# The prompt's latent attention moved between the steps of a delta-rule recurrence, in a two-layer decoder step

## The chip, the cores and the metric

The kernel runs as one program on one core of a Trainium2 chip. The metric is device time in microseconds, from the start to the end of one execution. The core has five engines with one in-order queue each: PE (TensorE), DVE (VectorE), ACT (ScalarE), POOL (GpSimd) and SP (SyncE, which here only issues DMAs). They meet through semaphores. PE writes its results to eight banks of PSUM, called banks below, and DVE or ACT empties them into SBUF.

## The reference, cut to what matters

One step of a decoder with two layers, for a prompt (16 meta tokens and 256 tokens, 272 positions) and for eight samples with one new token each and a past of 1024 positions. All is float32. The change is in the odd layer, whose mixer is two things side by side: an RWKV-7 recurrence with 8 heads of 64, and multi-head latent attention (MLA) with 8 heads.

```python
def step(S, inp):                                    # RWKV-7, per head
    r_t, w_t, k_t, v_t, a_t, b_t = inp
    sa = jnp.einsum('bhij,bhj->bhi', S, a_t)
    S = S * w_t[:, :, None, :] + sa[..., None] * b_t[:, :, None, :] + v_t[..., None] * k_t[:, :, None, :]
    return S, jnp.einsum('bhij,bhj->bhi', S, r_t)
...
q = (qa @ P['mla_w_qb'][i]).reshape(B, T, MLA_HEADS, QK_NOPE + QK_ROPE)     # 64 + 32 columns a head
q_nope, q_rope = q[..., :QK_NOPE], rope(q[..., QK_NOPE:], pos)
c, kr = rms_norm(ckv, P['mla_kv_norm'][i]), rope(kr, pos)                   # latent 256, rotary key 32
q_lat = jnp.einsum('bthn,chn->bthc', q_nope, P['mla_w_uk'][i])
# samples only: past_c, past_kr gathered from 64 pages of 128 positions, put ahead of c and kr
s = (jnp.einsum('bqhc,bkc->bhqk', q_lat, c) + jnp.einsum('bqhr,bkr->bhqk', q_rope, kr)) * MLA_SCALE
pr = jax.nn.softmax(jnp.where(k_pos <= q_pos, s, -jnp.inf), axis=-1)
y_d = jnp.einsum('bthc,chv->bthv', jnp.einsum('bhqk,bkc->bqhc', pr, c), P['mla_w_uv'][i])
mix = jnp.concatenate([y_c, y_d], -1) @ P['od_w_out'][i]                    # y_c is the recurrence's side
```

## The kernel before, in words

The queues' order is written out by hand: `odd_pe`, `odd_dve`, `odd_act`, `odd_pool` and `odd_sp` hold the odd layer's instructions for each engine. PSUM's eight banks are two rings of four (`Ring`, L150): V, emptied by DVE, and A, emptied by ACT. `claim` (PE) waits until a bank of the ring is free again, `take` (DVE or ACT) until the next one is full; a ring is served strictly in order.

**The recurrence.** The prompt's 272 positions are three tiles, of 128, 128 and 16 (the tuple PT, L542). For each tile and all eight heads, PE turns four token-major operands (L546), makes five pairs of products of 128 by 128 (L564), DVE masks them and sets up the inverse of a triangular matrix (ten masks, then six operations, on which PE waits), and four *levels* build that inverse: squares (L576), masked by DVE, then two products each (L583, L587), added by DVE. Behind the levels come a product with the values (`ak`, L592), the results of L600, L606 and L620, the outputs of the tile (L629, L630), and for each 32 positions one step of the state (L638, L642). PE and DVE wait on each other all the way; ACT and, after the sample part is done, POOL have almost nothing to do there.

**Behind the recurrence** stands the whole latent attention. First the state's store (L649) and the key matrix turned (L662); queries head by head into 64 rows of a bank (L670) and the rotary parts (L676); the recurrence's head means (L1536); keys per head (L698); its variances (L1536); values (L704); latents turned (L710 to L716); the samples' latent queries (L730) and scores with the new token (L738). Then follow the prompt's eight heads: scores (L744), softmax on DVE and ACT (L1054 to L1065, L1169), probabilities turned (L805), times values (L817). Between the heads, by the tables TURNED and SCORED (L146, L147), PE turns the samples' cached keys (L756, with one set of key buffers for each third of the 288 key rows) and makes their scores (L765). At the end stand the samples' probabilities, values (L790) and output (L834), and the output projection (L1603) with the mixture of experts behind it.

The cache's 64 pages (128 KB of latents each on SP's queue, L1297, and 16 KB of rotary keys on POOL's, L1263) are loaded into SBUF columns that the recurrence uses, so both queues wait until the recurrence's operands are dead, its states stored (`wkv_out`) and the latent queries made (`qlat`). The table of pages is read for 40 of them ahead of that wait, for the last 24 between the loads.

Of the kernel before, what the change touches and what calls it, by code (L numbers as in the profile page):

```python
# [27 lines left out]
P = 128  # L28
# [9 lines left out]
NPG = PAST // PAGE  # L38
ALPHA = 4.0 ** 0.25
# [106 lines left out]
TURNED = {2: [(0, 0)], 3: [(0, 1), (0, 2)], 4: [(1, 0), (1, 1)], 5: [(1, 2), (2, 0)], 6: [(2, 1), (2, 2)], 7: [(3, 0), (3, 1), (3, 2)]}  # L146
SCORED = {3: 0, 5: 1, 6: 2, 7: 3}  # L147
# [45 lines left out]
SCRATCH = 30820  # L193
# [26 lines left out]
def program(nc, a, outs):  # L220
    sems = {}

    with ExitStack() as ctx:
# [23 lines left out]
        h_full, h_free, g_full, g_free = sem("h_full"), sem("h_free"), sem("g_full"), sem("g_free")  # L247
        v_full, v_free, a_full, a_free = sem("v_full"), sem("v_free"), sem("a_full"), sem("a_free")
# [171 lines left out]
        kt_read = {}  # L420
# [39 lines left out]
        OSQ1, OSD1 = part(25872, 4, NT), part(26992, 4, NT)  # L460
        MIXR1, MIXS1 = part(28460, 4, NT), part(29580, 4, NT)

        CK = part(0, NB, NPG, 288)
        WUKT, QAN, CNF, KRR = part(0, MH, KVL), QA, CKV, KRF
        MSQ, MSK, MSD = part(22400, 3, NT), part(23240, 2, NT), part(16800, 2, NT)
        KT1, KT2, RT1, RT2 = part(17360, NT), part(17640, NT), part(6440, NT), part(6720, NT)
        QRF = part(7000, 2, NT)
        Q96, K96 = part(18432, MH, NT), part(20672, MH, NT)
        VM, CT9 = part(22912, 3, 512), part(24448, 3, 288)
        PTS = part(25872, 3, NPR)  # L470
        SCM = part(26688, 2, 3, NPR)
        STAT = part(28320, 2, 3, 4)
        QLP, QLF, CS8, C8T = resv(0, NB, 3, 32), resv(768, 3, 64), resv(960, 288), resv(1248, 3, NB)
# [3 lines left out]
        KT3 = [SLOT[:, HOME[n], :].rearrange("p (s t) -> p s t", s=4) for n in (S_MOE[1], S_ODO + 3, S_ODO + 2)]  # L477
        SCS = SLOT[:, HOME[S_ODO + 1], :].rearrange("p (g t) -> p g t", g=2)
        O8, PC, OLT, P8 = part(18432, 2, KVL), part(18944, 2, P), part(19200, 2, 2, P), part(20672, 2, NPG, P)
# [12 lines left out]
        def odd_pe(pe, V, A, close, until, slot, used, to_fm, project, fm_sums, out_and_moe):  # L492
# [40 lines left out]
            pe.wait_ge(ev("smp_cols"), 1)  # L533
            for q in range(6):
                b = A.claim()
                for m in range(4):
                    ins = pe.transpose(b[0:NB, P * m:P * m + P], SMP[:, q, m, :], ident)
                close(A, ins, "srow2")
# [1866 lines left out]
```

## Time and profile before

| | |
|---|---|
| median of 3 runs | 1148.06 us (1147.82 to 1151.13) |
| the profiled execution's own time | 1146.33 us |
| its span | 1144.6 us |
| PE busy | 988.4 us, 86% of the span |
| DVE busy | 484.6 us, 42% |
| ACT busy | 216.3 us, 19% |
| POOL busy | 138.0 us, 12% |
| mean granted TensorE clock | 0.879 of full speed |

The odd layer's stretch that the change touches runs from 582.9 us, the first tile of the recurrence, to 893.9 us, the output projection. The trace has, for each instruction, its start and duration, the idle time of its engine before it and which engine's event ended that. A window gives, for a stretch of time, how long each engine was busy and the mean clock granted to PE, as a share of full speed: 1.00 is 2.4 GHz, 0.50 is 1.2 GHz. A float32 matmul of the program is two recorded ones, so counts of PE in the trace are twice those of the program.

### The profile page before, as it was taken

Reading aid. Unit: us, or ns where it says so; the run is one execution under the profiler, and the core shown is the slowest. Engines: PE = TensorE matmul, PEld = TensorE weight load, DVE = VectorE, ACT = ScalarE, POOL = GpSimd, SP = SyncE. Lnnn points to the kernel's source line nnn. Section 1 sums busy time; section 2 is a strip of 40 time slices with the busy share of each in tenths; the row PEclk is TensorE's granted clock in tenths of the full one; section 3 lists DMA queues with packets and bytes.
Section 4 is the critical chain, followed back from the end, with each engine's and each line's share of the span. In section 5 each row is a group of like instructions: output and inputs, shape, how many; then the busy total and the mean of one; then the engine's idle time right before and its main releaser. Section 6 shows DMA issues by size and latency. Waiting matters only on the chain.

```text
span 1144.6 us, 17771 instructions
## 1 busy us (share of the span) xinstructions
PE 988.4 (86%) x7132; PEld 742.6 (65%) x7132; DVE 484.6 (42%) x1060; ACT 216.3 (19%) x462; POOL 138.0 (12%) x177
## 2 busy tenths in 40 slices
PE   6997478779799999899969778996888988999995
PEld 4775366557666666677759777754555767666674
DVE  1697723452431110214886675438663135111114
ACT  0112011201401101125520000031454032111103
POOL 0005001000040000000029600002720002200000
PEclk9998756779699999989989688596699987999998
DMA  9403101715169998032100100003722541999501
GB/s 310 168 24 37 34 1 42 265 42 198 60 254 385 394 400 242 1 120 89 53 14 1 40 1 2 7 1 113 204 64 74 184 184 51 376 389 398 220 1 38
DMA packets 77222, 156.88 MB, mean 137 GB/s; under 512 B 19605, under 2 KB 57549, under 8 KB 68215
## 3 DMA queue, kind: packets, MB, share of 16 engines
q1 hardware_dynamic: 67668, 148.28, 35.6%
q0 software_dynamic: 3760, 4.48, 1.8%
q10 hardware_dynamic: 5710, 2.96, 0.9%
q8 instruction: 58, 0.95, 0.3%
q14 instruction: 26, 0.21, 0.1%
HBM read 149.25 MB, written 5.27 MB: 135 GB/s over the span
## 4 chain that ended last, share of the span: by engine, by line
PE 70%; DVE 21%; DMA 3%; ACT 3%; issue 2%; SPq 0%; POOL 0%; DVEq 0%; ACTq 0%
PE bank L1686 10%; PE bank L1350 7%; DVE scratch L1772 7%; PE bank L1673 6%; PE bank L1746 5%; PE bank L1718 5%; PE bank L1603 5%; DVE scratch L1775 2%; PE bank L1464 2%; PE bank L576 2%; PE bank L1634 2%; PE bank L756 2%; DMA scratch<-u_tok_dram 1%; PE bank L1552 1%; PE bank L587 1%
## 5 line engine op out<-in xcount | busy, mean ns | idle before, releaser
L1350 PE MATMUL bank<-x_fm,weight_slots 128*128 128x280 f32 x576 | 143.0, 411 | 4.2 <-ACT x_fm L2228 2.8
L1350 PEld LDWEIGHTS bank<-x_fm,weight_slots 128*128 128x128 f32 x576 | 112.5, 196 | 32.9 <-issue 4.4
L2160 ACT ACTIVATE scratch<-bank 128x280 f32<-128x280 f32 (+5 forms) x118 | 52.9, 454 | 325.1 <-PE bank L1718 92.3
L1686 PE MATMUL bank<-weight_slots,scratch 128*64 128x256 f32 x672 | 92.5, 379 | 1.2 <-DVE scratch L1769 1.2
L1686 PEld LDWEIGHTS bank<-weight_slots,scratch 128*64 128x64 f32 x672 | 58.5, 137 | 27.8 <-issue 4.6
L1769 DVE COPY scratch<-bank 128x256 f32<-128x256 f32 (+5 forms) x108 | 55.9, 517 | 43.1 <-PE bank L1673 17.2
L1772 DVE TENSOR_TENSOR scratch<-scratch 128x64 f32<-128x64 f32 (+12 forms) x95 | 57.8, 626 | 33.9 <-ACT scratch L2160 31.4
L1673 PE MATMUL bank<-scratch 128*128 128x128 f32 x512 | 68.3, 289 | 0.0
L1772 DVE TENSOR_TENSOR scratch<-bank,scratch 128x256 f32<-128x256 f32 x16 | 6.8, 424 | 143.6 <-PE bank L1686 143.6
L1603 PE MATMUL bank<-scratch,weight_slots 128*128 128x280 f32 x256 | 63.5, 411 | 4.0 <-DVE scratch L1772 4.0
L1673 PEld LDWEIGHTS bank<-scratch 128*128 128x128 f32 x512 | 62.2, 199 | 4.1 <-issue 0.4
L1746 PE MATMUL bank<-scratch 128*128 128x280 f32 x256 | 60.9, 400 | 1.4 <-ACT scratch L2160 1.4
L1603 PEld LDWEIGHTS bank<-scratch,weight_slots 128*128 128x128 f32 x256 | 50.2, 197 | 17.0 <-DVE scratch L1772 4.4
L1746 PEld LDWEIGHTS bank<-scratch 128*128 128x128 f32 x256 | 48.5, 190 | 14.7 <-ACT scratch L2160 3.2
L1686 PE MATMUL bank<-scratch 128*64 128x256 f32 x352 | 56.9, 379 | 0.0
L1263 POOL DMA_DIRECT2D scratch<-in_cache_krope x64 | 34.4, 538 | 160.9 <-DVE residual L1017 143.6
L1686 PEld LDWEIGHTS bank<-scratch 128*64 128x64 f32 x352 | 35.7, 137 | 16.4 <-issue 3.4
L1207 POOL TENSOR_TENSOR scratch<-scratch 128x256 f32<-128x256 f32 x24 | 16.1, 704 | 241.3 <-DVE scratch L1772 241.3
L1464 PE MATMUL bank<-scratch 64*42 64x128 f32 x128 | 25.9, 418 | 22.1 <-DVE scratch L1775 22.1
L1718 PE MATMUL bank<-weight_slots,scratch 128*64 128x512 f32 x192 | 43.8, 598 | 0.3
L2221 ACT ACTIVATE scratch<-residual 128x280 f32<-128x280 f32 x32 | 11.7, 437 | 156.6 <-DVE residual L2018 156.6
L1772 DVE TENSOR_TENSOR scratch<-bank,consts 128x512 f32<-128x512 f32 (+5 forms) x69 | 33.7, 488 | 15.4 <-PE bank L576 11.7
(380 smaller groups left out, 1496.3 us busy)
## 6 DMA issues: line engine op xcount, KB each, us to landing
weight_slots<-in_moe_w_down SPq DMA_DIRECT2D x24, 1024.0 KB, 9.5
weight_slots<-in_moe_w_up SPq DMA_DIRECT2D x22, 1024.0 KB, 7.9
weight_slots<-in_moe_w_gate SPq DMA_DIRECT2D x20, 1024.0 KB, 7.2
scratch<-in_moe_w_gate SPq DMA_DIRECT2D x12, 1024.0 KB, 8.2
scratch<-in_moe_w_up SPq DMA_DIRECT2D x10, 1024.0 KB, 8.8
weight_slots<-in_od_w_in SPq DMA_DIRECT2D x9, 1024.0 KB, 5.8
weight_slots<-in_ev_w_in SPq DMA_DIRECT2D x8, 1024.0 KB, 11.9
scratch<-in_moe_w_down SPq DMA_DIRECT2D x8, 1024.0 KB, 10.0
```

Of the source, the lines that this page charges most:

```text
L576: ins = pe.matmul(heads(b, r)[:r, hp, :], NTM[:r, par, hp, 0:r], TM_[:r, par, hp, 0:r], start=True, stop=True)
L1263: pool.dma_start(CK[:, sm, pg, 256:288], a["cache_krope"][bass.ds(page[i], 1), 0].rearrange("o p c -> p (o c)")).then_inc(ev(f"cache_krope ...
L1350: ins = pe.matmul(b[:, 0:NT], w[:, k, P * m2:P * m2 + P], src[:, k, :], start=(k == 0), stop=(k == kt - 1))
L1464: ins = pe.matmul(b[0:HCOL, P * i:P * i + P], HS[lo:lo + SP_N, j, g // 2, :], CP[lo:lo + SP_N, j, g // 2, 1:CL + 1, :].rearrange("p l c -> ...
L1603: ins = pe.matmul(b[:, 0:NT], w[:, k0 + k, P * m2:P * m2 + P], src[:, k, :], start=(which == 0 and k == 0), stop=(which == 1 and k == 3))
L1673: ins = pe.matmul(b[:, f], XTM[:, t, 4 * half + c, :], slots(t, slice(0, P)), start=False, stop=(t == 1))
L1686: ins = pe.matmul(b[CAP * j:CAP * j + CAP, 0:DE], XG[:, q % 2, k, CAP * j:CAP * j + CAP], w[j][:, k, :], start=(k == 0), stop=(k == KD - 1))
L1718: ins = pe.matmul(b[CAP * j:CAP * j + CAP, :], HT[:, q % 2, f, CAP * j:CAP * j + CAP], w[j][:, f, 512 * h:512 * h + 512], start=(f == 0), ...
L1746: ins = pe.matmul(b[:, 0:NT], YG[:, q, P * m:P * m + P], DSPT[:, q, :], start=(q == 0), stop=(q == NQ - 1))
L1769: s.do(dve.tensor_copy(dst, src if len(dst.shape) == 2 else src.rearrange("p (a b) -> p a b", a=dst.shape[1])), v_free)
L1772: return dve.tensor_tensor(o, x, y, ALU.mult)
L2160: return act.activation(dst, b[:rows, 0:width], f, **kw).then_inc(ring.free, 1)
```

## The change

Nothing of the mathematics is changed; work is put in another place and other banks.

- During the recurrence ScalarE's ring is three banks (`W`), the fourth bank (`YB`) holds the tile's outputs. ACT also empties the turned operands and `ak`, which were DVE's.
- `beside(tt, k)` stands at 17 points of each full tile and 14 of the short one, in PE's, DVE's and ACT's code alike. In the first tile it issues everything of the latent attention up to the latent queries; queries and keys are made for two heads at once, in the bank's lower and upper 64 rows. In the second and third tile each head takes three points (`HEAD_POINTS`): scores, with the causal mask added by PE (identity times the mask) instead of DVE; the largest scores by DVE straight from the bank and the exponentials by ACT straight from the bank; the normalisation by DVE. The head before is turned at the first point and multiplied with the values at the second. Heads 0 to 5 fall in the second tile, 6 and 7 in the third.
- Behind the recurrence stands the samples' attention alone. Its pages' loads wait for the last tile's outputs being emptied (`y_free`), go in the order group, half, sample, page, with a semaphore for each half; the key buffers are four, used in turn by twelve pieces.
- The group norm of the recurrence (its scale is on DVE) stands beside the samples' key pieces.

```diff
-TURNED = {2: [(0, 0)], 3: [(0, 1), (0, 2)], 4: [(1, 0), (1, 1)], 5: [(1, 2), (2, 0)], ...
-SCORED = {3: 0, 5: 1, 6: 2, 7: 3}
+HEAD_POINTS = 3
+        WB, YB = AB[0:3], AB[3]
...
+            def queries(h):
+                w = slot_view(S_QB + h // 4, 3, 384)
+                b = W.claim()
+                for k in range(3):
+                    for i in range(2):
+                        c = 96 * (h % 4 + i)
+                        ins = pe.matmul(b[64 * i:64 * i + 64, 0:NT], w[:, k, c:c + 64], QAN[:, k, :], start=(k == 0), stop=(k == 2))
+                close(W, ins, "q_pairs")
...
+            def scores(h):
+                b = [W.claim(), W.claim()]
+                for t, o in ((0, 0), (2, 128), (1, 0)):
+                    c0, r = PT[t]
+                    to = b[t % 2][:r, o:o + c0 + r]
+                    pe.matmul(to, Q96[0:96, h, c0:c0 + r], K96[0:96, h, 0:c0 + r], start=True, stop=False)
+                    ins = pe.matmul(to[:, c0:c0 + r], ident[:r, 0:r], cst("causal")[:r, 0:r], start=False, stop=True)
...
+            def probs_turned(h):
+                pe.wait_ge(ev("p_ready"), 3 * h + 3)
...
+            def beside(tt, k):                                   # PE
+                if tt > 0:
+                    j = 17 * (tt - 1) + k
+                    h, part_ = j // HEAD_POINTS, j % HEAD_POINTS
+                    if part_ == 0 and 0 < h <= MH:
+                        probs_turned(h - 1)
+                    if part_ == 0 and h < MH:
+                        scores(h)
+                    if part_ == 1 and 0 < h <= MH:
+                        attend(h - 1)
+                    if j == 29:
+                        new_scores()
+                elif k == 0:
+                    sample_rows(0)
+                ...
+                elif k == 15:
+                    latent_queries()
...
+            def largest_scores(h):                               # DVE
+                b, full = score_banks[h]
+                dve.wait_ge(*full)
+                for t, o in ((0, 0), (1, 0), (2, 128)):
+                    s.mark(dve.tensor_reduce(STAT[:r, h % 2, t, 0:1], b[t % 2][:r, o:o + c0 + r], AX.X, ALU.max, negate=True), ev("s_ready"))
+            def normalised(h):
+                dve.wait_ge(ev("p_exp"), 3 * h + 3)
+                s.do(dve.reciprocal(STAT[:, h % 2, :, 2], STAT[:, h % 2, :, 1]))
...
+            def exps(h):                                         # ACT
+                b = [W.take(), W.take()]
+                act.wait_ge(ev("s_ready"), 3 * h + 3)
...
-            pool.wait_ge(*mark["qlat"])
-            pool.wait_ge(ev("wkv_out"), 16 * 2)
+            pool.wait_ge(y_free, len(PT))
...
+            keys_turned(0)                                       # PE, behind the recurrence
+            keys_turned(1)
+            fm_sums(OSQ1, cst("blk"), 4, False, "hn_var1", "hn_sq", A)
+            keys_turned(2)
+            keys_turned(3)
+            sample_scores(0)
+            ...
```

**PE, levels of the first tile.** The names are those of the operands' memories; 128x128 is what one instruction writes. Before:

```order
L576 MATMUL bank<-scratch 128x128 x8
L583 MATMUL bank<-scratch 128x128 x4
L587 MATMUL bank<-scratch 128x128 x4
L583 MATMUL bank<-scratch 128x128 x4
L587 MATMUL bank<-scratch 128x128 x4
L576 MATMUL bank<-scratch 128x128 x8
```

and in the same place of the changed kernel:

```order
L786 MATMUL bank<-scratch 128x128 x8
L575 MATMUL bank<-scratch,weight_slots 64x280 x6
L800 MATMUL bank<-scratch 128x128 x4
L804 MATMUL bank<-scratch 128x128 x4
L800 MATMUL bank<-scratch 128x128 x4
L804 MATMUL bank<-scratch 128x128 x4
L575 MATMUL bank<-scratch,weight_slots 64x280 x6
L584 MATMUL bank<-scratch,weight_slots 32x280 x12
L786 MATMUL bank<-scratch 128x128 x8
```

L786, L800 and L804 are L576, L583 and L587 of before. A pair of query heads (L575) now stands before the products and another, with the rotary parts (L584), behind them.

**DVE, the first two levels of the second tile.** Before:

```order
L1772 TENSOR_TENSOR scratch<-bank,consts 128x512 x2
L1775 TENSOR_TENSOR scratch<-scratch,bank 128x512 x4
L1772 TENSOR_TENSOR scratch<-bank,consts 128x512 x2
L1775 TENSOR_TENSOR scratch<-scratch,bank 128x512 x4
```

and after:

```order
L1079 TENSOR_REDUCE scratch<-bank 128x1 x2
L1079 TENSOR_REDUCE scratch<-bank 16x1
L2019 TENSOR_TENSOR scratch<-bank,consts 128x512 x2
L1084 RECIPROCAL scratch<-scratch 128x3
L1087 TENSOR_SCALAR weight_slots<-weight_slots,scratch 128x128
L1087 TENSOR_SCALAR weight_slots<-weight_slots,scratch 128x256
L1087 TENSOR_SCALAR weight_slots<-weight_slots,scratch 16x272
L2022 TENSOR_TENSOR scratch<-scratch,bank 128x512 x4
L2019 TENSOR_TENSOR scratch<-bank,consts 128x512 x2
L1079 TENSOR_REDUCE scratch<-bank 128x1 x2
```

The masks (L1772, now L2019) and sums (L1775, now L2022) of the levels have the largest scores of head 0, its normalisation and the largest scores of head 1 between them, each behind a wait in the same in-order queue.

**PE, behind the recurrence.** Before, the last key pieces and the samples' values:

```order
L756 MATMUL bank<-consts,scratch 96x128 x48
L765 MATMUL bank<-weight_slots,residual 32x512 x12
L817 MATMUL bank<-scratch 64x272
L817 MATMUL bank<-scratch 64x144
L817 MATMUL bank<-scratch 64x16
L788 MATMUL bank<-residual,scratch 32x256 x4
```

and after, from the group norm's variances on:

```order
L1783 MATMUL bank<-scratch,consts 128x280 x4
L893 MATMUL bank<-consts,scratch 96x128 x32
L903 MATMUL bank<-weight_slots,residual 32x512 x12
L893 MATMUL bank<-consts,scratch 96x128 x48
L903 MATMUL bank<-weight_slots,residual 32x512 x12
L893 MATMUL bank<-consts,scratch 96x128 x48
L913 MATMUL bank<-consts,scratch 128x128 x8
L916 MATMUL bank<-consts,residual 8x128
L903 MATMUL bank<-weight_slots,residual 32x512 x12
L893 MATMUL bank<-consts,scratch 96x128 x32
L903 MATMUL bank<-weight_slots,residual 32x512 x12
```

The prompt's heads are gone from between the key pieces (L756, now L893) and the samples' scores (L765, now L903); the first group's probabilities (L913) stand before the third scores.

## Rows read from the trace of the kernel before

**Rows 1.** The page's part on the chain that ended last: shares by engine.

```profile
PE 70%; DVE 21%; DMA 3%; ACT 3%; issue 2%; SPq 0%; POOL 0%; DVEq 0%; ACTq 0%
```

**Rows 2.** Windows: start:end, length, busy of PE, PEld, DVE, ACT, POOL, PE clock, DMA share, GB/s.

```profile
582.90:648.60 65.70, 52.55 (x706) 49.84 (x703) 41.48 (x62) 2.92 (x7) 51.58 (x51) 0.80 0.08 23
648.60:709.70 61.10, 49.70 (x691) 47.19 (x690) 38.53 (x62) 0.60 (x1) 0.53 (x1) 0.86 0.01 2
709.70:737.00 27.30, 23.06 (x451) 20.79 (x450) 14.67 (x50) 0.60 (x1) 0.00 (x0) 0.63 0.01 2
737.00:792.90 55.90, 45.63 (x250) 28.66 (x249) 29.30 (x39) 15.07 (x33) 0.00 (x0) 0.84 0.04 9
792.90:878.30 85.40, 74.91 (x484) 45.33 (x484) 45.82 (x149) 41.98 (x107) 34.42 (x64) 0.82 0.42 124
878.30:893.90 15.60, 12.37 (x200) 7.29 (x196) 5.77 (x11) 1.92 (x5) 0.00 (x0) 1.00 0.77 270
```

**Rows 3.** Short windows, the same columns.

```profile
640.00:644.00 4.00, 2.45 (x46) 2.45 (x48) 1.85 (x4) 0.00 (x0) 3.84 (x3) 0.50 0.62 262
778.00:784.00 6.00, 6.00 (x50) 5.95 (x51) 5.57 (x2) 0.00 (x0) 0.00 (x0) 0.61 0.19 54
816.00:820.00 4.00, 4.00 (x19) 3.54 (x20) 2.97 (x11) 2.35 (x7) 2.18 (x4) 0.50 0.58 167
```

**Rows 4.** Timeline of PE, first tile: start, duration, line, operands, count, idle before.

```profile
599.33 3.75 PE L576 MATMUL bank<-scratch 128*128 128x128 f32 x16 [6.05 <-DVE scratch L1775]
...
641.55 1.12 PE L638 MATMUL bank<-scratch 64*64 64x64 f32 x16 [3.17 <-DVE scratch L1775]
```

**Rows 5.** Timeline of PE, from the rotary parts to the new scores.

```profile
747.37 1.62 PE L676 MATMUL bank<-scratch,weight_slots 128*32 128x280 f32 x24
...
760.09 7.76 PE L698 MATMUL bank<-scratch,weight_slots 128*64 128x280 f32 x32
...
769.77 5.42 PE L704 MATMUL bank<-weight_slots,scratch 128*128 128x512 f32 x12
...
777.98 0.31 PE L720 MATMUL bank<-consts,residual 8*96 8x8 f32 x3 [1.33 <-DVE residual L1769]
778.22 6.10 PE L730 MATMUL bank<-scratch 64*96 64x8 f32 x48
792.86 1.42 PE L738 MATMUL bank<-residual 96*32 96x8 f32 x48 [8.55 <-DVE residual L1019]
```

**Rows 6.** Timeline of ACT at the fourth query head and the rotary parts.

```profile
747.48 0.40 ACT L2160 ACTIVATE scratch<-bank 64x280 f32<-64x280 f32 x1 [1.02 <-PE bank L670]
749.06 0.40 ACT L2160 ACTIVATE scratch<-bank 128x280 f32<-128x280 f32 x1 [1.19 <-PE bank L676]
```

**Rows 7.** Timeline of PE: one prompt head and what stands behind it.

```profile
839.52 1.13 PE L817 MATMUL bank<-scratch 128*64 128x272 f32 x6
840.57 1.49 PE L744 MATMUL bank<-scratch 96*128 96x128 f32 x6
841.99 1.04 PE L805 MATMUL bank<-consts,scratch 128*128 128x128 f32 x6
842.96 1.95 PE L756 MATMUL bank<-consts,scratch 128*96 128x128 f32 x16
...
847.23 2.78 PE L765 MATMUL bank<-weight_slots,residual 96*32 96x512 f32 x24
```

**Rows 8.** DVE by line and form, 792 to 895: busy, mean ns, idle before.

```profile
L1056 DVE TENSOR_REDUCE scratch<-scratch 128x1 f32<-128x256 f32 x8 | 3.4, 420 | 0.3
```

**Rows 9.** ACT by line and form, the same stretch.

```profile
L1169 ACT ACTIVATE scratch<-scratch 128x256 f32<-128x256 f32 x8 | 4.1, 510 | 5.5 <-DVE scratch L1056 5.5
```

**Rows 10.** Timelines of SP and POOL: the page loads, and POOL's last.

```profile
792.48 48.83 SPq L1297 DMA_DIRECT2D scratch<-in_cache_kv  x64
...
844.14 0.53 POOL L1263 DMA_DIRECT2D scratch<-in_cache_krope  x1 [0.60 <-issue]
```

**Rows 11.** DMA issues, 737 to 895: count, KB each, median us to landing.

```profile
scratch<-in_cache_krope POOLq DMA_DIRECT2D x64, 16.0 KB, 2.7
```

More of the change, by code:

```diff
@@ L38 @@
 NPG = PAST // PAGE
+PAGES = [(4 * g + j, 4 * half + i) for g in range(2) for half in range(2) for j in range(4) for i in range(4)]
 ALPHA = 4.0 ** 0.25
@@ new lines, in values, with latents_turned @@
+            def values(t):
+                c0, r = TT[t]
+                b = W.claim()
+                for k in range(2):
+                    ins = pe.matmul(b[:r, :], CNF[:, k, c0:c0 + r], uv[:, k, :], start=(k == 0), stop=(k == 1))
+                close(W, ins, "vm")
+            def latents_turned(c0, r, name):
+                b = W.claim()
+                for k in range(2):
+                    pe.transpose(b[:r, P * k:P * k + P], CNF[:, k, c0:c0 + r], ident)
+                ins = pe.transpose(b[:r, 256:384], KRR[:, c0:c0 + r], ident)
+                close(W, ins, name)
@@ L607, in odd_pe @@
                 close(V, ins, "re")
+                beside(tt, 11)
                 until("tv")
@@ new lines, in new_scores, with beside @@
+            def new_scores():
+                b = V.take()
+                s.do(add(SCUR, b[:, 0:2 * NB].rearrange("p (g t) -> p g t", g=2), cst("curmask").rearrange("p (g t) -> p g t", g=2)), v_free)
+                for g in range(2):
+                    s.do(dve.tensor_reduce(STS[:, g, 1:2], SCUR[:, g, :], AX.X, ALU.max, negate=True))
+            def beside(tt, k):
+                if tt > 0:
+                    j = 17 * (tt - 1) + k
+                    h, part_ = j // HEAD_POINTS, j % HEAD_POINTS
+                    if part_ == 1 and h < MH:
+                        largest_scores(h)
+                    if part_ == 2 and h < MH:
+                        normalised(h)
+                    if j == 28:
+                        latent_queries()
+                    if j == 29:
+                        new_scores()
+                elif k == 9:
+                    queries_turned()
@@ new lines, in keys, with rotary_rows @@
+            def keys(h):
+                b = W.take()
+                act.activation(K96[0:64, h, :], b[0:64, 0:NT], ACT.Copy)
+                act.activation(K96[0:64, h + 1, :], b[64:128, 0:NT], ACT.Copy).then_inc(w_free, 1)
+            def rotary_rows():
+                for h in range(MH):
+                    if h % 4 == 0:
+                        act.wait_ge(ev("qr_sum"), h // 4 + 1)
+                    act.activation(Q96[64:96, h, :], QRF[32 * (h % 4):32 * (h % 4) + 32, h // 4, :], ACT.Identity, scale=SCALE).then_inc(ev("q_rope"), 1)
@@ L1191, in odd_act @@
+            keys_turned(0)
+            keys_turned(1)
+            std(OSD1, WD, 64e-5, 4)
+            for n in range(2, 9):
+                keys_turned(n)
+            sample_exps(0)
+            for n in range(9, 12):
+                keys_turned(n)
             sample_exps(1)
```

669 lines of the change are left out of this document (380 added, 289 removed).

## The prediction, made before the changed kernel ran

> **What bounds the kernel now.** The first view is the chain that ended last: it passes through PE for 70% of the span and DVE for 21% [rows 1]. So what counts is what PE executes and what it waits for from DVE. The second is a table of windows, one for each stage of the odd layer [rows 2]. Three rows are the recurrence's tiles (65.7, 61.1 and 27.3 us), in which PE is busy 52.55, 49.70 and 23.06 us, hence idle 13.2, 11.4 and 4.2; ACT works 4 us in all three together. Then 55.9 us of projections, 85.4 us of prompt heads with the samples' keys, and 15.6 us of samples' values before the output projection at 893.9. The third view is the PE clock in the same rows: 0.80, 0.86 and 0.63 in the tiles, and PE has only two levels there, 0.50 and 1.00 (a 4 us window with PE busy 2.45 shows 0.50 [rows 3]). A mean of 0.80 is 40% of the time at half, so half clock holds about 26 us of tile 0, 17 of tile 1 and 20 of tile 2, 63 us together. The fourth is PE's timeline: the gaps are waits for DVE, 6.05 us before the first level of a tile and 3.17 before the state steps [rows 4]. The levels themselves leave little idle at full clock: what is put there is mostly added to the tile.
>
> So the change fills few holes. Its gain, if any, must come from what moving makes cheaper, and from page loads that start nearer to the recurrence's end.
>
> **Tile 0, what it gains.** Queries: ACT's rows give 1.42 us a head (1.02 idle and 0.40 busy [rows 6]). In pairs the two 64-column products stand in different halves of the array. No row shows two of 64 columns, but L676 shows 24 products of four 32-column parts in 1.62 us [rows 5], which is one head's price, so they run beside each other. I take a pair at one head's price: 4 x 1.42 = 5.7 us (11.3 if they don't overlap). Rotary parts 2 x 1.6 = 3.2. Keys, 7.76 [rows 5], also in pairs: 3.9. Two turned rotary parts are four recorded products of 280 columns at 7.76/32: 0.9. Values 5.4. Latents turned: between 769.77 + 5.42 = 775.19 and the idle 1.33 before 777.98 lie 1.5 us, 12 transposes. The wait of 1.33 stays, since it is one hand-over. Latent queries 6.10 at a mean clock of 0.61, most of it half [rows 3]; at full about 3.1. The key matrix turned, eight transposes by the same price: 1.0. Sum 26.0 us, and 1 for hand-overs between the two kinds of work: **+27**. The evictions are ACT's, idle here, so they cost PE nothing as long as three banks suffice: a 280-column one takes 0.40 us [rows 6], PE's product for it 1.4.
>
> **Tile 1.** Each head costs PE scores 1.42, turning 0.97 and values 1.05, from the starts of the rows 839.52 to 842.96 [rows 7]. The mask is now three small products more; DVE's addition of it goes. It has no row: by the scores' own rate (1.42 us for 128, 256 and 272 columns, 656 in all) its 272 columns are 0.6, and by the transposes' 0.12 for 128 columns 0.3. I take 0.46. Six scores, five turnings and five values: 6 x 1.88 + 5 x 0.97 + 5 x 1.05 = 21.4. Some of it falls in the waits of 6.05 and 3.17: -2. The new waits between engines: +3, because a head has three points, each some 61.1/17 = 3.6 us apart before and 5 after, for a chain of three reductions (at most 0.42 each [rows 8]), three exponentials (0.51 and a read of the sum behind each [rows 9]) and the normalisation, some 4.5 us in all spread over 15. DVE's load grows from 38.5 by about 2.4 a head, less five evictions: some 50 of 83 us. **+22.4**.
>
> **Tile 2.** Two scores, three turnings, three values and the samples' new scores (1.42 [rows 5]): 3.8 + 2.9 + 3.2 + 1.4 = 11.3. The short tile's points were 27.3/14 = 2 us apart, so the same chain of 4.5 us doesn't fit between them; for three heads' ends I add 8 of waits. **+19.3**.
>
> **The clock.** Of 63 us at half clock PE is busy some 47. All of it at full would save 24; a gap that stays keeps its half clock. I take a quarter: **-6** (bounds 0 and -24). Growth 27 + 22.4 + 19.3 - 6 = 63, so the recurrence ends at 737 + 63 = 800.
>
> **Behind it.** Page loads start with the last tile emptied, and by the rows of before SP takes 48.83 us to issue them and POOL issues its last at 844.14, 51.7 us after SP's first, landing 2.7 later [rows 10, 11]: 55 us. Under it run the first nine key pieces (16 transposes each, 2.0 us, and scores at 2.8 [rows 7]: 9 x 2.0 + 2 x 2.8 = 24), and the group norm, which is mostly DVE's, idle otherwise. So the loads are the bound: PE has under half of the 55 us to do. Then what needs the last quarter: last transposes of piece 9 0.5, the first group's probabilities 1.3, scores 2.8, pieces 10 and 11 4.1, scores 2.8: 11.5. PE has waited before it, and behind its two waits in the profile (8.55 us at 792.86 among them [rows 5]) the clock was still 0.50 from 816 to 820, with PE busy throughout [rows 3]; of 11.5 us I take a quarter at twice the time: +3. Then the tail of the row 878.30:893.90, less the last head's 1.05: 14.5. Sum 55.6 + 11.5 + 3 + 14.5 = 84.6, against 893.9 - 737 = 156.9 before. Output projection at 884.6, **9.3 us earlier**. Where it comes from: pairs 9.5, latent queries at full clock 3, the wait of 8.55 for them and their page loads gone from the path, 6 of clock; against them stand DVE's waits of the heads and loads that are no longer covered by anything.
>
> The profiled execution took 1146.33 with a span of 1144.6; the median is 1148.06. I take the gain off the median: 1148 - 9 = 1139, and because the bound on the clock is one-sided I name 1138.
>
> The Trainium skill ("TensorEngine Tiling (Array Packing)", section Key Properties) says "Mode switching requires drain", which speaks against putting products of 64 or 32 columns between the recurrence's. Its row here: from the last 64-column head to the four 32-column parts ACT's spacing is 1.59 instead of 1.42 [rows 6], 0.17 us for one switch, against the 1 us for hand-overs in tile 0. Some 40 switches at 0.17 would be 7 us, 5 more than the sum has.
>
> **Rivals.**
> A, the sum: 1138, between 1128 and 1144.5.
> B, the interleave absorbs more. PE idles 28.8 us in the tiles, and 63 us are at half clock. If half the idle and half of the 24 us are recovered, growth falls from 63 to about 45 and the time to 1120. For: engines' waits are hand-overs that side work fits into. Against: at full clock the levels have no holes, and the gaps of 6.05 and 3.17 come where few points stand.
> C, slower: the head's chain in the in-order queues. DVE waits at a head's third point for all three exponentials, with the level's masks and sums queued behind it, for which PE waits; PE waits at the next point for the normalisation, with the level's products behind it. A chain not hidden at all is 4.5 us of work and 0.5 of hand-overs, 40 us for eight heads where the sum has 11. At 4 us a head the growth is 84 and the time 1159. It decides once the recurrence grows by over 72. For: points differ in length, and several lie within 3 us. Against: 15 us for a chain of 5 in tile 1.
> D, no net: the pairs don't overlap (5.6 for queries, 3.9 for keys), which gives 9.5 back: 1148. For: the two products of a pair have a hand-over in the array that L676's row doesn't show. Against: that row.
> E, switches at 0.17 us: 1143. It is inside A's range.
>
> **How the numbers follow.** A 0.45 (with E), B 0.23, C 0.22, D 0.10. The measurement tells no change from about 0.3%, 3.4 us, so the same is 1144.6 to 1151.5: D and an edge of C. Faster 0.66, same 0.12, slower 0.22. The range takes B to 1114 (growth 39: half the waits and most of the clock) and C to 1162; the forecast's own is 1128 to 1147.
>
> **What would show it.** Windows of the changed kernel: tiles of 88 to 93, 80 to 86 and 43 to 48 us, clock up to 0.85 to 0.9; the pairs of queries at 1.4 us; PE idle before the first turning of each head under 1 us in tile 1 and 2 to 3 in tile 2; SP's loads beginning within 1 us of the last tile's end and PE idle, released by DMA, before piece 9; 84 us from the last tile to the output projection. Wrong, if the recurrence grows by under 50 or over 72, if the loads take another time than 55, or if PE waits behind the last page for something else than pages.

## The result, and the profile after

| | before | changed |
|---|---|---|
| median of 20 runs each | 1148.83 us | 1142.23 us |
| ratio | | 0.9934, 95% interval 0.9917 to 0.9952 |
| profiled execution (its span) | 1146.33 (1144.6) | 1143.98 (1142.3) |

Ratios, here and below, leave out single executions that were clearly slower than the rest of their kernel; medians don't.

The change saves 0.66%, 7.6 us of the 1148.06 that the forecast started from (5.5 to 9.5 by the interval). The forecast was 10 us. The size is right; where it comes from is only in part as forecast.

The windows of the changed kernel that answer to [rows 2] are its three tiles and the stretch from the recurrence's end to the output projection:

```profile
582.60:670.30 87.70, 77.59 (x942) 61.04 (x942) 46.10 (x67) 26.12 (x60) 52.37 (x52) 0.93 0.07 22
670.30:758.40 88.10, 76.09 (x821) 64.33 (x820) 45.43 (x96) 16.19 (x56) 0.00 (x0) 0.86 0.01 1
758.40:803.50 45.10, 41.07 (x557) 31.43 (x558) 17.65 (x69) 8.98 (x28) 0.00 (x0) 0.56 0.01 2
803.50:887.70 84.20, 64.00 (x510) 41.31 (x510) 27.99 (x36) 32.19 (x63) 34.53 (x64) 0.78 0.57 177
```

With each tile counted from its first transpose (583.03, 648.54 and 709.66 before), the tiles grew by 22.2, 27.0 and 17.7 us, 66.9 in all where the forecast had 63. Their clock went from 0.80, 0.86 and 0.63 to 0.93, 0.86 and 0.56. Behind the recurrence 84.2 us are left of 156.9; the forecast had 84.6. So the output projection starts at 887.7 instead of 893.9. Of those 6.1 us this execution gives 3.8 back, most of it in the output projection: 128 recorded products take 33.29 us there instead of 30.45, since PE begins them at half clock (0.50 from 887.74 to 892.00; before, the first 4.1 us of them are at 1.00).

PE's timeline of the changed kernel in the second tile shows one head at full clock (turning, then scores L651 and mask L652, then later the values):

```profile
701.23 0.99 PE L665 MATMUL bank<-consts,weight_slots 128*128 128x128 f32 x6
702.15 0.49 PE L651 MATMUL bank<-weight_slots 96*128 96x128 f32 x2
702.48 0.39 PE L652 MATMUL bank<-consts 128*128 128x128 f32 x2
702.79 0.63 PE L651 MATMUL bank<-weight_slots 96*16 96x272 f32 x2
703.36 0.21 PE L652 MATMUL bank<-consts 16*16 16x16 f32 x2
703.50 0.70 PE L651 MATMUL bank<-weight_slots 96*128 96x256 f32 x2
704.03 0.39 PE L652 MATMUL bank<-consts 128*128 128x128 f32 x2
704.25 1.95 PE L786 MATMUL bank<-scratch 128*128 128x128 f32 x16
```

Scores with mask take 704.25 - 702.15 = 2.10 us where scores alone were 1.42 [rows 7]: the mask adds 0.68, not 0.46 (0.58 against the kernel without a mask, tried below, whose scores take 1.52). The same rows in the third tile, and what follows them:

```profile
763.73 0.76 PE L651 MATMUL bank<-weight_slots 96*128 96x128 f32 x2
764.28 0.63 PE L652 MATMUL bank<-consts 128*128 128x128 f32 x2
764.84 1.09 PE L651 MATMUL bank<-weight_slots 96*16 96x272 f32 x2
...
767.04 0.63 PE L652 MATMUL bank<-consts 128*128 128x128 f32 x2
767.60 0.61 PE L786 MATMUL bank<-scratch 16*16 16x16 f32 x16
771.22 1.94 PE L675 MATMUL bank<-scratch,weight_slots 128*64 128x272 f32 x6 [1.30 <-ACTq L1335]
```

The reader is to see the starts: 767.60 - 763.73 = 3.87 us for the same work, with no wait in it. The clock is 0.50 from 767.60 to 803.40, although PE is busy 32.57 of those 35.80 us. The waits that the heads bring into this tile, 1.30 the longest, are 2.6 us in all.

Behind the recurrence the chain that ended last runs over SP's queue. L1543 is the load, L1542 the reading of a page's number from the table:

```profile
840.08 0.33 SPq L1543
840.42 0.05 issue
840.46 0.27 SPq L1542
840.76 0.15 SPq L1542
...
841.17 0.33 SPq L1543
```

One page takes 1.09 us, of which the load is 0.33. POOL's queue, with the rotary keys, is as slow: 1.14 us a page, 0.54 of it the load. POOL even ends last. It issues its last load at 855.65, SP's last latents have landed at 854.23, and PE goes on at 858.41; so the last wait is most likely POOL's, which the profile doesn't name. PE stands idle for the pages: of its waits in this stretch the largest is on the key pieces, five times, 15.2 us.

```profile
PE bank L893 <- issue: 15.2, 5, 4.6
PE bank L926 <- DVE scratch L1199: 1.7, 1, 1.7
```

### The profile page after: what moved, and what is told of

Its sections match the earlier page's. It is cut to its first block, busy times and chain, and to the rows that moved or that the text cites. A ratio compares the mean times of both kernels' runs of the same rounds, so it can differ in the third digit from the quotient of the medians.

```text
span 1142.3 us, 17732 instructions
## 1 busy us (share of the span) xinstructions
PE 996.6 (87%) x7172; PEld 746.4 (65%) x7172; DVE 444.9 (39%) x952; ACT 234.9 (21%) x512; POOL 138.5 (12%) x177
## 4 chain that ended last, share of the span: by engine, by line
PE 70%; DVE 18%; SPq 3%; issue 3%; ACT 3%; DMA 2%; DVEq 0%; ACTq 0%
PE bank L1933 10%; PE bank L1597 7%; DVE scratch L2019 7%; PE bank L1920 6%; PE bank L1993 5%; PE bank L1850 5%; PE bank L1965 5%; DVE scratch L2022 2%; PE bank L1711 2%; SPq L1543 2%; PE bank L1658 2%; PE bank L786 2%; PE bank L1881 2%; PE bank L651 1%; PE bank L1799 1%
## 5 line engine op out<-in xcount | busy, mean ns | idle before, releaser
L2407 ACT ACTIVATE scratch<-bank 128x280 f32<-128x280 f32 (+5 forms) x118 | 55.5, 479 | 330.3 <-PE bank L1965 92.3
L2019 DVE TENSOR_TENSOR scratch<-scratch 128x64 f32<-128x64 f32 (+12 forms) x95 | 57.8, 627 | 33.0 <-ACT scratch L2407 30.5
L1850 PE MATMUL bank<-scratch,weight_slots 128*128 128x280 f32 x256 | 66.6, 425 | 3.8 <-DVE scratch L2019 3.8
L2019 DVE TENSOR_TENSOR scratch<-bank,scratch 128x256 f32<-128x256 f32 x16 | 6.8, 425 | 143.9 <-PE bank L1933 143.9
L2016 DVE COPY scratch<-bank 128x256 f32<-128x256 f32 (+4 forms) x87 | 42.1, 484 | 29.9 <-PE bank L1920 17.7
L2019 DVE TENSOR_TENSOR scratch<-bank,consts 128x512 f32<-128x512 f32 (+5 forms) x69 | 33.7, 488 | 42.0 <-PE bank L786 23.1
```

The costliest lines, as they stand in the source:

```text
L1850: ins = pe.matmul(b[:, 0:NT], w[:, k0 + k, P * m2:P * m2 + P], src[:, k, :], start=(which == 0 and k == 0), stop=(which == 1 and k == 3))
L2016: s.do(dve.tensor_copy(dst, src if len(dst.shape) == 2 else src.rearrange("p (a b) -> p a b", a=dst.shape[1])), v_free)
L2019: return dve.tensor_tensor(o, x, y, ALU.mult)
L2407: return act.activation(dst, b[:rows, 0:width], f, **kw).then_inc(ring.free, 1)
```

## The experiments

Ratios are to the kernel before, run beside each; the changed kernel has 0.9934. Differences between two kernels are differences of ratios, times 1148.

**Two heads behind the recurrence.** `BESIDE` heads stay between the steps, the rest follow the recurrence on ScalarE's ring of four.

```diff
+BESIDE = 6
-                    if part_ == 0 and h < MH:
+                    if part_ == 0 and h < BESIDE:
                         scores(h)
...
             fm_sums(YW, cst("blk"), 4, False, "hn_mean", None)
+            for h in range(BESIDE, MH):
+                probs_turned(h, A)
+                attend(h, A)
+                if h + 2 < MH:
+                    scores(h + 2, A)
```

> The changed kernel with heads 6 and 7 taken out of the tile of 16 positions and put directly behind the recurrence, under the page loads, two heads in flight on ScalarE's ring of four. Theory 1 (what the trace of the changed kernel says of that tile): it runs at half clock from end to end, so two heads and a half cost 18 us there where they are 10 at full clock, and they delay the page loads, which then leave PE idle 17 us. Expected: third tile 45.1 us down to 24 to 29, page loads 16 to 20 us earlier, out-projection 13 to 18 earlier, time 1142 down to 1125 to 1130. Rival (the heads' chains, some 8 us each, push all key pieces back so that PE and not the page loads sets the end): third tile as short, but only 0 to 6 us of it left at the out-projection.

Measured: 1126.66 us, ratio 0.9779 (0.9739 to 0.9820), 18 us faster than the changed kernel.

```profile
761.00:790.50 29.50, 27.01 (x508) 23.34 (x508) 13.87 (x55) 4.32 (x10) 0.00 (x0) 0.58 0.01 2
790.50:875.80 85.30, 71.52 (x559) 47.06 (x559) 31.60 (x50) 36.06 (x81) 34.39 (x64) 0.80 0.57 175
```

The third tile is 29.5 us instead of 45.1, and the stretch behind it 85.3 instead of 84.2: two heads more in it cost 1.1 us, since PE waited for pages anyway. Of those waits one of 4.3 us is left, and here the profile names what ended it: the rotary keys of POOL's queue. Theory 1 holds, though the tile is half a microsecond longer than its 24 to 29.

**Page loads dealt out to both queues.** Each queue issues 64 loads as before, but for 32 pages only, whose numbers it reads ahead of the wait.

```diff
-            for n, (sm, pg) in enumerate(PAGES):
+            for n, (sm, pg) in enumerate(PAGES[0::2]):
...
-                if n >= EARLY_PAGES:
-                    page.append(sp.value_load(PTAB[0:1, i:i + 1], ...))
+                sp.dma_start(CK[sm][:, pg, 256:288], a["cache_krope"][...])
                 sp.dma_start(CK[sm][:, pg, 0:256], a["cache_kv"][...])
```

> The changed kernel with the pages' loads dealt out otherwise: SP issues latents and rotary keys of every second page, POOL those of the others, so each queue knows its 32 pages ahead of the wait and no page number is read between the loads. Theory 1: the 55 us of the page window are issue time, 0.5 us a load plus 0.6 us for each of the last 24 page numbers on both queues; expected first load to last landing 38 to 44 us instead of 55, PE less idle, out-projection 7 to 12 us earlier, time 1130 to 1135. Rival: the window is set by what the transfers themselves take (DMA share 0.85 to 0.95 at its start) or POOL needs longer for a load of 128 KB than for one of 16 KB; then the window shrinks by under 4 us and the time by under 3.

Measured: 1129.83, ratio 0.9832 (0.9789 to 0.9875), 12 us faster. POOL issues its last load 37.7 us behind its first, and PE's last wait for a page ends 45.2 us behind SP's first load instead of 54.5. Behind the recurrence 74.1 us are left instead of 84.2. So the page window was issue time, as theory 1 says, and what went from it are the page numbers read between the loads: by POOL's rows 24 gaps of about 0.60 us, 14 of the 51.2 us that its issues took. The rest, the loads' own issue, stays. The window is a little longer than the 38 to 44 expected: PE goes on only 6.5 us behind POOL's last issue (2.2 in the changed kernel). The DMA engines are at a share of 0.92 there (835 to 845), where they were at 0.48 (835 to 850), so what the transfers take begins to show; that they are the cause of the 6.5 is not shown.

**Loops of queries and keys exchanged.**

```diff
-                for k in range(3):
-                    for i in range(2):
+                for i in range(2):
+                    for k in range(3):
                         c = 96 * (h % 4 + i)
```

> The changed kernel with the two loops of queries and keys exchanged: all products of one head, then all of the other, in the same bank, so two products in different halves of the array never follow each other directly. Same work, same banks. Theory (the pairs run beside each other, 1.56 us for a pair of query heads in the trace): first tile 5.7 + 3.9, some 9 to 10 us longer, time 1149 to 1152. Rival (forecast as D: no overlap, a pair is two heads' price or the gaps hide it): no change within 2 us.

Measured: 1143.26, ratio 0.9945 (0.9914 to 0.9976), no change that can be told. The edit did not do what it was meant to: a pair of query heads went from 1.56 us only to 2.09, two pairs of key heads stayed at 2.08. The likely reading is that products still overlap where the second head's first follows the first head's last. So it says nothing on rival D.

**No mask.**

```diff
-                    pe.matmul(to, Q96[0:96, h, c0:c0 + r], K96[0:96, h, 0:c0 + r], start=True, stop=False)
-                    ins = pe.matmul(to[:, c0:c0 + r], ident[:r, 0:r], cst("causal")[:r, 0:r], start=False, stop=True)
+                    ins = pe.matmul(to, Q96[0:96, h, c0:c0 + r], K96[0:96, h, 0:c0 + r], start=True, stop=True)
```

> The changed kernel without the causal mask's products on PE (the prompt's scores are not masked: this part of the computation is left out). The forecast gave the mask 0.46 us a head, 3.7 us in all. The trace of the changed kernel shows 0.68 at full clock and 1.4 at half (scores and mask 2.10 and 3.84 where scores alone were 1.42), so theory 1: 6 to 8 us less, most of it in the second and third tile. Rival: the scores' end is not waited for at once, so the mask's price is smaller than its busy time, 0 to 3 us.

Measured: 1136.15, ratio 0.9879 (0.9841 to 0.9916), 6.3 us faster: theory 1. The second tile fell from 88.1 to 83.4 us, the third from 45.1 to 42.0.

**All heads behind the recurrence** (`BESIDE = 0`).

> The changed kernel with all eight prompt heads directly behind the recurrence, under the page loads, two in flight; the first tile's pieces stay where they are. It asks what the heads between the recurrence's steps bring at all. Theory 1 (they fill no holes: in the second tile they added 27.0 us for 24.8 us of PE work, in the third 17.8): the recurrence ends 42 to 45 us earlier, at about 760; behind it PE has 8 heads at 5 to 5.5 us, 6 of norm, 36 of key pieces and scores, 1.3 and the tail of 14.5, no longer waiting for pages: 102 us, output projection at 862 to 870 against 887.8, time 1118 to 1125, like or better than two late heads. Rival (the heads' chains can't be overlapped with only two in flight: 8 us a head as scores, maximum, exponentials, normalisation, turning in a row): 125 us behind the recurrence, output projection at 885 to 890, time 1140 to 1145, no change from the changed kernel.

Measured: 1159.85, ratio 1.0099 (1.0068 to 1.0130), 19 us slower than the changed kernel. The rival came true, and worse. But the recurrence tells what was asked:

```profile
667.10:728.80 61.70, 48.37 (x689) 45.89 (x688) 34.85 (x57) 3.37 (x6) 0.00 (x0) 0.88 0.01 2
728.80:756.60 27.80, 23.83 (x500) 21.73 (x496) 13.16 (x52) 3.13 (x6) 0.00 (x0) 0.59 0.01 3
```

Without heads the second and third tile are 61.7 and 27.8 us, those of [rows 2] again. So the heads cost 88.1 - 61.7 = 26.4 us in the second tile, 4.4 a head, for 27.7 us that PE is busy more; and 17.3 in the third, where PE is busy 17.2 us more. In sum they filled next to nothing. In detail they filled old waits and brought new ones. First the rows without heads:

```profile
707.59 3.79 PE L817 MATMUL bank<-scratch 128*128 128x64 f32 x32 [0.85 <-DVE scratch L2050]
723.09 0.95 PE L859 MATMUL bank<-scratch 64*64 64x64 f32 x16 [2.16 <-DVE scratch L2050]
```

then the same two places of the changed kernel, and its two new waits:

```profile
727.78 3.68 PE L813 MATMUL bank<-scratch 128*128 128x64 f32 x32
746.51 0.77 PE L855 MATMUL bank<-scratch 64*64 64x64 f32 x16
751.48 1.04 PE L665 MATMUL bank<-consts,weight_slots 128*128 128x128 f32 x6 [0.43 <-DVE weight_slots L1087]
758.44 2.02 PE L760 MATMUL bank<-consts,scratch 128*16 128x128 f32 x16 [1.61 <-ACTq L1335]
```

Waits of 0.85 and 2.16 us are gone, 0.43 and 1.61 are new. The wait of 6.05 before the first level is the same in both.

Behind the recurrence a head took 10.1 us, as PE's timeline shows:

```profile
783.20 1.55 PE L668 MATMUL bank<-consts,weight_slots 128*128 128x128 f32 x6 [1.98 <-DVE weight_slots L1098]
785.45 1.94 PE L679 MATMUL bank<-scratch,weight_slots 128*64 128x272 f32 x6 [0.70 <-issue]
787.32 0.80 PE L653 MATMUL bank<-weight_slots 96*128 96x128 f32 x2
...
793.29 1.55 PE L668 MATMUL bank<-consts,weight_slots 128*128 128x128 f32 x6 [1.99 <-DVE weight_slots L1098]
```

Of a head's 10.1 us 2.7 are waits (1.98 and 0.70) and 7.4 work at half clock.

**Four heads behind the recurrence** (`BESIDE = 4`).

> The changed kernel with heads 0 to 3 between the steps of the second tile and heads 4 to 7 behind the recurrence. Theory 1: recurrence ends at 803.4 - 18 - 9 = 776, PE behind it 4 x 5.3 + 6 + 36 + 1.3 + 14.5 = 79 plus half clock at its start, 83; the page loads take 55 plus 11.5, 3 and 14.5: 84. Both limits meet: output projection at 860 to 865, time 1114 to 1120, better than two late heads (1127) by 6 to 12. Rival (chains of 8 us a head): 94 us behind the recurrence, output projection at 870, time 1125, like two late heads.

Measured: 1132.38, ratio 0.9848 (0.9820 to 0.9876): 8 us slower than with two. The recurrence took 193.8 us and the stretch behind it 101.7, against 205.8 and 85.3. Both the 1114 to 1120 of theory 1 and the rival's 1125 were missed. PE waits for no page any more; four late heads no longer fit under them.

**The mask in bfloat16.**

```diff
-                    ins = pe.matmul(to[:, c0:c0 + r], ident[:r, 0:r], cst("causal")[:r, 0:r], start=False, stop=True)
+                    ins = pe.matmul(to[:, c0:c0 + r], M16[:r, 0:r], M16[:r, P:P + r], start=False, stop=True)
...
+            s.do(dve.tensor_copy(M16[:, 0:P], ident))
+            s.do(dve.tensor_copy(M16[:, P:2 * P], cst("causal")))
```

> The changed kernel with the mask's products (identity times causal mask) in bfloat16, which both hold exactly enough; scores, softmax and everything else unchanged. Theory 1 (a float32 product passes the array more often than a bfloat16 one, and the mask is on the path): most of what leaving the mask out gave (1142 to 1136) comes back, 4 to 6 us. Rival (the price is the change of the weights and the second accumulation, not the passes): 0 to 2 us.

Measured: 1141.96, ratio 0.9949 (0.9927 to 0.9971), no change that can be told. In the trace the mask of a head costs about half:

```profile
704.63 0.49 PE L652 MATMUL bank<-weight_slots 96*128 96x128 f32 x2
704.95 0.22 PE L653 MATMUL bank<-scratch 128*128 128x128 bf16 x1
705.11 0.63 PE L652 MATMUL bank<-weight_slots 96*16 96x272 f32 x2
705.67 0.17 PE L653 MATMUL bank<-scratch 16*16 16x16 bf16 x1
705.77 0.70 PE L652 MATMUL bank<-weight_slots 96*128 96x256 f32 x2
706.30 0.22 PE L653 MATMUL bank<-scratch 128*128 128x128 bf16 x1
706.37 2.17 PE L785 MATMUL bank<-scratch 128*128 128x128 f32 x16
```

Scores and mask take 1.74 us instead of 2.10, 3 us in eight heads. The tiles were 92.3, 80.9 and 43.0 us: shorter in the two that have heads, but 4.6 longer in the first, ahead of which this edit only adds DVE's two copies, and where the clock was 0.88 instead of 0.93. How the half-clock stretches fall differs from one execution to the next by more than this edit is worth; whether it gains 3 us stays open.

**One head a bank, all in the lower half.**

```diff
-                b = W.claim()
-                for k in range(3):
-                    for i in range(2):
-                        ins = pe.matmul(b[64 * i:64 * i + 64, 0:NT], w[:, k, c:c + 64], ...)
+                for i in range(2):
+                    b = W.claim()
+                    for k in range(3):
+                        ins = pe.matmul(b[0:64, 0:NT], w[:, k, c:c + 64], ...)
```

> The changed kernel with one head of queries and of keys a bank, all in the lower 64 rows, as before the change (exchanging the loops alone left neighbouring products in different halves of the array, and they still overlapped: 2.09 us for a pair of query heads instead of 1.56, keys as before). Theory (pairs overlap): 1.42 us a query head and 0.97 a key head, so the first tile grows by 5.1 for the queries and 3.7 for the keys, 9 us, and the time to 1149 to 1152, no faster than the kernel before. Rival D: no change within 2 us, since PE waits for other engines there.

Measured: 1145.10, ratio 0.9981 (0.9951 to 1.0010), 5.4 us slower. Rows of PE's timeline, first of this kernel (a pair of query heads, two pairs of key heads), then of the changed one:

```profile
615.77 3.04 PE L575 MATMUL bank<-scratch,weight_slots 128*64 128x280 f32 x12
...
642.27 3.99 PE L593 MATMUL bank<-scratch,weight_slots 128*64 128x280 f32 x16
```

```profile
612.84 1.64 PE L575 MATMUL bank<-scratch,weight_slots 128*64 128x280 f32 x12
614.40 1.16 PE L800 MATMUL bank<-scratch 128*128 128x128 f32 x8
...
633.70 2.11 PE L593 MATMUL bank<-scratch,weight_slots 128*64 128x280 f32 x16
```

By the starts, 2.97 us against 1.56 for a pair of query heads and 3.92 against 2.04 for two pairs of keys: 4 x 1.41 + 2 x 1.88 = 9.4 us of work. Pairs overlap, rival D falls: by these rows, not by the time. The time was expected at 1149 to 1152 and shows 5.4 us with an interval of some 3 us about it; the first tile is 5.9 us longer, at a clock of 0.96 instead of 0.93, which hides a part.

**All heads behind the recurrence, queues in another order.** The turned probabilities go through VectorE's ring, and VectorE normalises the next head before it takes the largest scores of the one behind. The edit is shown against the run before with all heads late.

```diff
             for h in range(BESIDE, MH):
-                probs_turned(h, A)
+                probs_turned(h, V)
                 attend(h, A)
...
-                normalised(h)
+                b = V.take()
+                s.do(dve.tensor_copy(PTS[:, 0:416], b[:, 0:416]))
+                if h + 1 < MH:
+                    normalised(h + 1)
                 if h + 2 < MH:
                     largest_scores(h + 2)
```

> All eight heads behind the recurrence as in the run that took 1160, with their queues in another order: the turned probabilities go through VectorE's ring, and VectorE normalises head h+1 before it takes the largest scores of head h+2, so two heads are really in flight. Cause 1 (in that run a head took 10.1 us because VectorE's and ScalarE's orders let one head move at a time, and PE's waits kept it at half clock): a head falls to 5 to 7 us, the stretch behind the recurrence from 145.6 to 105 to 122 us, time 1118 to 1136. Rival (the chain of one head sets the pace whatever the order, or half clock does): 8 us a head or more, time above 1140.

Measured: 1147.68, ratio 1.0004 (0.9982 to 1.0025), 11 us faster than in the old order. PE's timeline:

```profile
780.52 1.50 PE L668 MATMUL bank<-consts,weight_slots 128*128 128x128 f32 x6
782.94 1.94 PE L679 MATMUL bank<-scratch,weight_slots 128*64 128x272 f32 x6 [0.93 <-issue]
784.81 0.80 PE L653 MATMUL bank<-weight_slots 96*128 96x128 f32 x2
...
788.59 1.50 PE L668 MATMUL bank<-consts,weight_slots 128*128 128x128 f32 x6
```

The order of the queues was 2 us of a head's 10.1: the wait of 1.98 is gone and 8.07 is left, 0.93 of it a wait. The other 7.1 us are work at half clock, as this stretch from the recurrence's end to the first key piece shows:

```profile
755.40:829.50 74.10, 62.72 (x211) 37.54 (x209) 25.42 (x79) 13.88 (x56) 34.40 (x64) 0.50 0.46 130
```

PE is busy 62.72 of 74.10 us, and the clock is 0.50 throughout. The rival is right.

**Two late heads with the loads dealt out, in the old and in the new order of the queues, and four late heads in the new one.** These are the edits above put together.

> Heads 6 and 7 behind the recurrence and the page loads dealt out to both queues without page numbers read between them. With two late heads PE waited 4.3 us for the last pages and was idle or at half clock before, so theory 1: the loads no longer bound anything, PE does, and the stretch behind the recurrence falls from 85.3 to 78 to 81 us, time 1127 down to 1120 to 1123. Rival (the two gains add, 15.5 and 12.5 us): 1115. Other rival (the loads never bound behind two late heads): 1126.

Measured: 1122.86, ratio 0.9785 (0.9757 to 0.9812): the same as two late heads alone (0.9779). PE's wait for pages (4.3 us) is gone in the trace and the stretch behind the recurrence is 81.3 us instead of 85.3, but the runs don't show it. Between theory 1 and "no gain" this stays open; that the two gains add is excluded.

> The same with the order of the late heads' queues mended as in the run before last. Two late heads took 25 us from the recurrence's end to the first key piece, with waits of 3.0, 0.7 and 0.7 us. Theory 1 (order of the queues): 3 to 5 us less, 1116 to 1119. Rival: with only two heads the order of their queues decides nothing, no change within 2 us.

Measured: 1117.89, ratio 0.9745 (0.9718 to 0.9772), the fastest kernel of this study: 2.6% below the kernel before, 22 us below the changed one. It is 4.6 us below the run before it, by intervals that overlap a little; its stretch behind the recurrence is 79.65 us.

```profile
783.10:862.75 79.65, 67.48 (x558) 44.72 (x558) 33.28 (x54) 34.81 (x77) 34.32 (x64) 0.85 0.61 188
```

> The same with four heads behind the recurrence. Theory 1 (a late head costs 5 to 6 us, one in the third tile 8.7, one in the second 4.4): heads 4 and 5, which stand in the second tile at full clock, cost more behind the recurrence at half clock than between its steps: time 2 to 4 us above the run with two late heads. Rival (late heads keep PE busy, the clock rises and the pages hide them): 2 to 6 us below it.

Measured: 1128.21, ratio 0.9816 (0.9785 to 0.9848), 8 us above two late heads. The sign is theory 1's, the size larger: a late head at half clock is 8.1 us, one in the second tile 4.4.

## Why the prediction was right in size, and where its steps were wrong

The growth of each tile can be split by the starts of PE's rows: the products that are new in it, the recurrence's own products, and PE's idle time (us, changed minus before).

| tile | forecast | measured | new products | the recurrence's own | idle |
|---|---|---|---|---|---|
| first | +27 | +22.2 | 29.6 | -4.4 | -3.1 |
| second | +22.4 | +27.0 | 24.8 | +1.6 | +0.6 |
| third | +19.3 | +17.7 | 18.7 | -0.8 | -0.2 |
| clock, all three | -6 | in the rows above | | | |
| sum | 63 | 66.9 | 73.1 | -3.6 | -2.7 |

**First tile, right in size.** The products that the forecast lists took 26.5 us for its 24.7: the values 7.0 instead of 5.4, the latent queries 2.0 instead of 3.1. Pairs overlap (the two runs on it); a pair of query heads costs 1.56 us and one of key heads 1.02, instead of 1.42 and 0.97. Left out of the list are the samples' 24 turned rows, which stood ahead of the tile before and stand in it now:

```profile
580.41 2.78 PE L537 MATMUL bank<-consts,scratch 128*8 128x128 f32 x24 [1.90 <-DVE scratch L931]
```

```profile
585.81 1.72 PE L549 MATMUL bank<-consts,scratch 128*8 128x128 f32 x12
594.28 1.48 PE L549 MATMUL bank<-consts,scratch 128*8 128x128 f32 x12
```

They are 3.0 us. Ahead of the tile they save little: it begins only 0.4 us earlier, behind a wait of 2.68 for DVE. Against all this stand 3.1 us less of waits (6.05 fell to 4.12 before the first level, because these rows and the key matrix are turned in it, and 3.17 to 2.30) and 4.4 of the clock.

Of the 1.56 us, 0.14 are more than one head's 1.42 and may be the change between products of 128 and of 64 columns. The Trainium skill ("TensorEngine Tiling (Array Packing)", Key Properties) says that a change of tiling mode drains TensorE. The rows are in line with it, but no run has the change alone. Some 40 changes, the forecast's count, would be an estimated 6 us of the 67.

**Second tile, too small: +27.0 for 22.4.** The waits were forecast about rightly: 2 us to fall into old ones and 3 of new ones, where 2.2 us of waits before the state steps are gone, 2.0 are new (0.4 in the tile, 1.6 at its end) and others grew by 0.7. The failed term is the work, "6 x 1.88 + 5 x 0.97 + 5 x 1.05 = 21.4". It took 24.8: the mask is 0.68 instead of 0.46 a head, 1.3 us in six, and the scores of the first and the fifth head ran mostly at half clock, 2.68 and 3.45 us instead of 2.10, 1.9 more. The recurrence's own products took 1.6 us more too.

**Third tile, right in sum by luck, wrong in cause: +17.7 for 19.3.** The forecast added 11.3 us of work at full clock and 8 of waits. The new products took 18.7 us, since those of the heads, all but the first turning, ran at half clock or close to it. The waits that are new are 2.6, and as much of the old ones went, so idle time did not grow at all. Two errors of 7.4 and 8 us cancel. The step "for three heads' ends I add 8 of waits" failed, and so did the price at full clock. It matters for what one does next: more buffers or a better order could have gained at most those 2.6 us there, taking two heads out gained 18 us.

**The clock.** One term of -6 for all three tiles does not hold. The recurrence's own products came out 3.6 us shorter in sum, 4.4 of it in the first tile. The time at half clock, estimated from the windows' means, is 12, 25 and 40 us where it was 26, 17 and 20: 77 us instead of 63. The first tile rose from 0.80 to 0.93, the second kept 0.86, the third fell from 0.63 to 0.56 although PE was busier. What decides where they fall no run shows.

**Behind the recurrence, right:** 84.2 for 84.6. Loads start 0.5 us behind its end, PE's last wait for pages ends 54.5 us behind the first load for a forecast of 55, and the remaining 29.3 us fit its 29.0. That the loads are the bound is shown by dealing them out. One reading was off: PE was to have under half of the 55 us to do, and it was busy 37.95 of 54.90, at a mean clock of 0.75. That leaves 17 us, room for two more heads and not for four.

**Left out.** The sum ended at the output projection. In this execution 3.8 us more are lost behind it; in nine of the twelve kernels tried the same 128 products took 30.45 us again, with the same work around them, in the other three 31.7 to 33.3. So it seems to belong to the execution and not to the change; with one profiled execution of each kernel this is not shown.

**Rivals.** B (more absorbed) is excluded by the tiles: PE idles 26.1 us in them where it idled 28.8. C (chain in the in-order queues) did not come in the tiles, where heads start 12 to 14 us apart in the second (the first two 28); it did come where heads stand close together, behind the recurrence: there an order that lets one head move at a time cost 2 of 10.1 us a head. D fell with the last run on pairs.

## What to carry to other kernels

Before work is moved between the steps of a recurrence, see whether those steps leave PE idle at the points that are chosen, and at which clock they run: work of another kind at a half-clock place costs up to twice as much (3.87 us against 2.10 for a head's scores here), and if a load waits for the end of that place, it delays the load as well. A stretch that is bound by loads is the better place for it, until its idle time is used up (here two heads of eight). And look at what a load's issue consists of: 0.33 us of load with 0.76 of table reading beside it is mended by giving each queue so few pages that it can read their numbers ahead.

## What the runs showed of the hardware

- PE stayed at 0.50 for 74 us while it was busy for 85% of them (62.72 of 74.10), and, in the third tile of the changed kernel, for 36 us while it was busy for 91% of them (32.57 of 35.80).
- Products of 64 columns in different halves of the array overlap also when they don't alternate: a pair of query heads took 1.56 us alternating, 2.09 one head after the other, 2.97 in the same half; for keys 2.04, 2.08 and 3.92 for two pairs.
- A bfloat16 product adds into a bank in which float32 products began, at 0.22 us for 128 by 128 where the float32 one took 0.39, and the kernel's results stay right.
- A load of 128 KB costs POOL's queue as much to issue as one of 16 KB does, 0.5 to 0.6 us; on SP's queue either costs 0.33.
